# A two-block transformer kernel on one core: VectorE takes the conditioning tiles at every other step of a chunk

## The reference, cut to what matters

```
# block 1, feed-forward: D_FF = 5632
h = rmsnorm(x, pre_ffn_g)
u = causal_dwconv(h @ w_up, conv_w, conv_b)      # w_up: 2048 x 11264, 3 taps over tokens
gate, val = split(u)
x = x + rmsnorm((gelu(gate) * val) @ w_down, post_ffn_g)

# block 2, its six modulation vectors: w_ada is 2048 x 12288 (100 MB)
m = silu(cond) @ w_ada + b_ada                   # cond: one vector; shift, scale and gate, twice
h = rms_norm(x, norm_w) * (1 + scale) + shift
...
x = x + g_m * (relu(hm @ w_mlp_up) ** 2 @ w_mlp_down)
```

## Time and profile before

| | |
|---|---|
| median of three executions | 2182.85 us |
| the profiled execution | 2189.57 us |
| its span, first to last instruction | 2187.9 us |
| TensorE busy | 2153.1 us, 98% |
| VectorE busy | 1529.7 us, 70% |
| ScalarE busy | 1085.6 us, 50% |
| GpSimd busy | 133.3 us, 6% |
| read from HBM | 483.00 MB, 222 GB/s over the span |

### The profile page before, as it was taken

One profiled execution on the slowest core, in us unless ns is written; L12 is line 12 of the kernel. 1 busy time (PEld: TensorE's weight loads), 2 busy tenths in 40 slices (PEclk: granted clock), 3 DMA queues, 4 the chain that ended last, 5 costly groups with the idle time before them and its releaser, 6 DMA issues.

```text
span 2187.9 us, 32356 instructions
## 1 busy us (share of the span) xinstructions
PE 2153.1 (98%) x10220; PEld 1780.4 (81%) x10220; DVE 1529.7 (70%) x1906; ACT 1085.6 (50%) x1458; POOL 133.3 (6%) x233
## 2 busy tenths in 40 slices
PE   8999999999999999999999999999999999999998
PEld 7888888888778888788888878888888888888876
DVE  7997779787897887867877554566555655555656
ACT  6545654655334554345588465464434434444434
POOL 2110000100010000100000000000000000000000
PEclk9999899999999999999999999999999999999999
DMA  9887077788898888978666541558667766766653
GB/s 331 290 271 251 3 246 245 252 269 276 259 289 268 276 270 265 308 237 265 220 218 195 174 154 49 176 170 273 209 194 231 221 194 205 240 194 210 227 172 111
DMA packets 279982, 487.05 MB, mean 223 GB/s; under 512 B 26252, under 2 KB 118740, under 8 KB 278560
## 3 DMA queue, kind: packets, MB, share of 16 engines
q1 hardware_dynamic: 249472, 371.42, 51.9%
q0 software_dynamic: 30192, 113.72, 17.1%
q10 hardware_dynamic: 176, 0.08, 0.0%
HBM read 483.00 MB, written 2.11 MB: 222 GB/s over the span
## 4 chain that ended last, share of the span: by engine, by line
PE 95%; ACT 2%; DVE 1%; issue 1%; DMA 0%; POOL 0%; ACTq 0%; POOLq 0%
PE G L1883 28%; PE G L1885 28%; PE G L1884 28%; PE T L2151 1%; PE T L2303 1%; PE T L2072 1%; ACT w_hi L583 1%; PE G L2052 1%; PE T L1917 1%; PE G L2283 1%; PE T L2097 0%; PE T L1965 0%; PE T L2099 0%; PE T L2098 0%; PE G L1980 0%
## 5 line engine op out<-in xcount | busy, mean ns | idle before, releaser
L1096 DVE TENSOR_TENSOR w_lo<-raw,w_hi 128x1024 fp32r<-128x1024 f32 (+1 forms) x704 | 849.0, 1216 | 445.1 <-ACT w_hi L583 442.3
L583 ACT ACTIVATE w_hi<-raw 128x1024 fp32r<-128x1024 f32 (+1 forms) x704 | 740.2, 1055 | 818.4 <-PE G L1885 812.0
L1883 PE MATMUL G<-w_hi,h_hi 128*128 128x512 f32 (+1 forms) x1656 | 648.1, 391 | 3.2 <-DVE h_lo L1181 1.9
L1885 PE MATMUL G<-w_hi,h_lo 128*128 128x512 f32 (+1 forms) x1656 | 642.4, 388 | 0.6 <-issue 0.6
L1884 PE MATMUL G<-w_lo,h_hi 128*128 128x512 f32 (+1 forms) x1656 | 641.7, 387 | 0.0
L1883 PE MATMUL G<-w_hi,a_hi 128*128 128x512 f32 x1120 | 440.7, 394 | 10.4 <-issue 6.8
L1885 PE MATMUL G<-w_hi,a_lo 128*128 128x512 f32 x1120 | 436.9, 390 | 0.0
L1884 PE MATMUL G<-w_lo,a_hi 128*128 128x512 f32 x1120 | 436.6, 390 | 0.0
L1883 PEld LDWEIGHTS G<-w_hi,h_hi 128*128 128x128 f32 x1656 | 311.5, 188 | 67.7 <-issue 6.6
L1885 PEld LDWEIGHTS G<-w_hi,h_lo 128*128 128x128 f32 x1656 | 311.1, 188 | 64.3
L1884 PEld LDWEIGHTS G<-w_lo,h_hi 128*128 128x128 f32 x1656 | 311.4, 188 | 61.5
(11 more groups left out here) (280 smaller groups left out, 1245.6 us busy)
## 6 DMA issues: line engine op xcount, KB each, us to landing
ada_w<-in_w_ada POOLq DMA_DIRECT2D x192, 512.0 KB, 5.0
raw<-in_w_up SPq DMA_DIRECT2D x352, 256.0 KB, 4.4
raw<-in_w_mlp_up SPq DMA_DIRECT2D x256, 256.0 KB, 2.9
raw<-in_w_mlp_down SPq DMA_DIRECT2D x256, 256.0 KB, 3.4
raw<-in_w_in SPq DMA_DIRECT2D x224, 256.0 KB, 4.0
raw<-in_w_down SPq DMA_DIRECT2D x176, 256.0 KB, 4.7
raw<-in_w_out SPq DMA_DIRECT2D x128, 256.0 KB, 3.8
raw<-in_w_in SPq DMA_DIRECT2D x16, 136.0 KB, 3.5
```

What stands on the lines that cost most here:

```text
L583: act.activation(w_hi[:, s % 4, :, 0:width], raw[:, s % 8, :, 0:width], ACT.Copy).then_inc(hi_ready, 1)
L1096: dve.tensor_tensor(w_lo[:, s % 4, :, 0:width], raw[:, s % 8, :, 0:width], w_hi[:, s % 4, :, 0:width].bitcast(F32), ALU.subtract).then_inc ...
L1883: pe.matmul(out, ah, wh, start=f, stop=False)
L1885: mm = pe.matmul(out, al, wh, start=False, stop=l)
```

## The change

`body` no longer spreads the tiles evenly over the steps that it has left. A table gives, for each number of tiles in a chunk, the steps behind whose low part they stand; they no longer keep to k of 4 and above in a chunk with taps and product.

| tiles in the chunk | before | after |
|---|---|---|
| 4, with taps and product | 4, 5, 6, 7 | 1, 3, 5, 7 |
| 4, without | 0, 1, 2, 3 | 1, 3, 5, 7 |
| 3 (up1c) | 4, 5, 6 | 1, 4, 6 |
| 2 (second feed-forward part) | 4, 5, or 0, 1 in a group's first chunk | 1, 5 |
| 1 (first chunk of up1c) | 0 | 4 |
| 6 (first chunk of up1b) | 0 to 5 | 0, 1, 3, 4, 6, 7 |
| the chunks that start at k = 5 | 5, 5, 6, 7 and 5, 6 | the same |

The tiles keep their order, the folds their steps, and no other stream is touched.

```
+        TILE_AT = {1: (4,), 2: (1, 5), 3: (1, 4, 6), 4: (1, 3, 5, 7), 6: (0, 1, 3, 4, 6, 7)}
+
         def body(s, d=0, post=None, n=8, adas=(), k0=0, fold=()):
 
-            adas = list(adas)
+            at = {2: (5, 6), 4: (5, 5, 6, 7)}[len(adas)] if k0 else TILE_AT.get(len(adas), ())
             for k in range(k0, n):
                 lo(s + 3 + k, d)
                 for at_, v, half in fold:
                     if at_ == k:
                         ada_fold(v, half)
-                if post and k == 2:
-                    post[0]()
-                elif post and k == 3:
-                    post[1]()
-                elif not post or k >= 4:
-                    left = n - k if not post else n - max(k, 4)
-                    for _ in range(-(-len(adas) // left)):
-                        ada_op(*adas.pop(0))
+                if post and k in (2, 3):
+                    post[k - 2]()
+                for a, op in zip(at, adas):
+                    if a == k:
+                        ada_op(*op)
```

## The result

| | before | after |
|---|---|---|
| median | 2183.61 us (2181.55 to 2188.32, 6 runs) | 2170.52 us (2169.48 to 2173.88, 6 runs) |
| ratio | | 0.9938, 95% interval 0.9924 to 0.9952 |
| span of the profiled execution | 2187.9 us | 2167.7 us |

The kernel after is 0.6% faster, 13.1 us by the medians; 2172 were forecast. The spans of the two profiled executions differ by 20.2 us, and that number must not be read as the gain. Both kernels run the same instructions up to the first transposes of up1a, and there the one before had already lost 7.4 us: they start at 407.37 in it, and at 399.93 in the kernel after. The windows over the attention of the first block show why (the row's columns are those of the earlier trace rows, with the granted clock third from the end).

What follows compares the result with a forecast made beforehand. TensorE, busy 98% of the span, was taken as the bound, losing time to VectorE's order. Gaps of -13.5 us and a fold wait of +2.2 gave -11.3, taken as -10.8 from 2182.85: 2172 us, range 2168 to 2181.

Steps and rivals of the forecast that it cites:

- The bound, and the loads behind the gaps: Whole kernel: TensorE sets the end; VectorE's 78.8 us of waits for tile loads cause TensorE's gaps, 13.5 us at stake.
- the gap at 548: Up1a: a TensorE gap of 0.54 us before a matmul at 548.03, expected to go, worth 0.8 us.
- The yardstick: Step costs: TensorE 2.72 us a step; VectorE 1.14 for a low part, 2.39 for a two-instruction tile, 1.20 for one.
- the 5.6 us of allowed lateness: Feed-forward steps: VectorE may be 5.6 us late with its low parts before TensorE waits.
- Down1a, -8.4: Down1a, 16 two-instruction tiles: VectorE enters on time, no gap is left, about 8.4 us saved.
- The fold in up1b, +2.2: Up1b's first chunk: the fold before step 3 newly waits 2.3 us for late tiles, costing 2.0 to 2.6, taken as 2.2.
- the case that holds it: Rival at up1b's fold: wait of 2.9 us and half clock behind it, total -9.4 us, 2173.5 us; chance 0.12.
- Up1a, -0.8, and down1b, -4.5: Up1a loses its one gap, 0.8 us; down1b's gaps come of loads alone and go, 4.5 us.
- Up1c and the second feed-forward part, 0: Up1c and the second feed-forward part: no gaps in the rows, so nothing gained; 0, bounds -0.5 to +1 us.
- The sum: All stages: -13.5 + 2.2 = -11.3 us on the profiled execution; -10.8 taken for the runs' median.
- quick loads: Rival: unprofiled loads land in 3.7 us, VectorE hardly waits before the change; gain only 2 us, 2181 us; chance 0.15.
- The slower rival: Chunks with taps, 14: early tiles meet a late VectorE, 1.2 us lost in each, total 2202 us; chance 0.05.

Runs made afterwards that it cites:

- e5: Kernel before, with the 112 tiles from up1a to up1c taken but not loaded and no wait for loads; 0.9945 of before, down1a 117.97 us.
- e6: Kernel after, with the same 112 tiles from up1a to up1c taken but not loaded; 0.9930 of before, down1a 115.77 us.
- e3: Kernel before, with the new tile steps in the up chunks of all three groups and none in the down chunks; 0.9968 of before.
- e1: Kernel before, with the new tile steps in the four chunks of down1a alone; 0.9987 of before (interval takes in 1), down1a 123.25 us.
- e4: Kernel after, with the second part's fold in up1b's first chunk moved from steps 3 and 5 to 5 and 7; 0.9931 of before.
- e9: Kernel after, with the tiles of down1a's last chunk at k = 0, 2, 4, 6; 0.9948 of before, fold wait 0.65 us.
- e7: The kernel after again, unchanged: a slip left the intended new steps unused, so it serves as a repeat; 0.9941 of before, down1a 115.78 us.
- e8: The kernel after again, unchanged: a slip left the intended new steps unused, so it serves as a repeat; 0.9938 of before, down1a 117.43 us.
- e10: Kernel after, with the four tiles of a chunk that has taps at k = 0, 1, 2, 3; 0.9986 of before, 2177.4 us.
- e2: Kernel before, with the new tile steps in down1b alone; 0.9986 of before (interval takes in 1), down1b 116.53 us.

## Why the prediction was right

*The bound, and the loads behind the gaps.* Right. 3.57 us of idle time in down1b and the gap at 548 are gone, VectorE's waits fell from 78.8 to 2.9 us (under 15 forecast), and e5 and e6 show that it is the loads. In down1a they hold the larger part and the row of tiles the rest, as the working had it. The waits were counted from 407 us on, and so the forecast misses the one that loads cause ahead of the first transposes; the change leaves it as it was.

*The yardstick* held: 3.5 us for a tile of two and a low part is the distance of e3's gaps, and the 5.6 us of allowed lateness gave e3's 4.7 us and e1's 3.4 us ahead of time (4 to 5 and 3 expected).

*Down1a, -8.4.* Without the fold it has no gap left, as forecast. The length fell by 5.4 us, 122.75 to 117.39. With the fold out of the way (e4, 113.37) it is 9.4 us shorter, and 0.5 of these are the old fold's wait: 8.9 for the term of 8.4.

*The fold in up1b, +2.2.* The wait is 2.23 us in the profile after, where the working gave 2.3 without a late load; against 0.27 that is +2.0. The place, the tile at k = 7, is shown by e9. The part of it that e4 gives back is 2.4 us, against 0.5 before: +1.9. I left the half clock out of the forecast, with a chance of 0.12 for the case that holds it. Of six profiled executions with this wait of 2.2 us (after, e1, e6, e7, e8, e10) four have it and two don't: 117.4 against 115.8 us for down1a. That it should come only where two gaps stand close together was wrong.

*Up1a, -0.8, and down1b, -4.5.* Measured -0.99 and -4.91. That the loads alone cause the gaps of down1b is right (e5). Where they do it was half right: by e2 and e3, one profile each, a part of the lateness came with VectorE out of up1b, and not from the tiles inside the stage. In the whole change both go, so the sum didn't notice.

*Up1c and the second feed-forward part, 0.* Up1c went from 113.37 to 113.33 us; in the rest of the kernel, 1107.6 us before and 1106.2 after, no gap came or went that a tile ends.

*The sum.* The stages from up1a to up1c fell by 11.3 us in the profiled pair, the forecast's own sum. That they agree so closely is luck: the gaps were worth 14.8 us where 13.5 were put at stake, the fold took back 1.9 instead of 2.2, and the half clock, left out of the sum, took back 1.6. Without it the stages would have fallen by 12.9. (A slip in the working hardly matters: it counts restarts for 10 gaps, none of them the fold's, and then takes the fold's 0.24 out of their sum.) The medians say 13.1, with an interval of 10.5 to 16.6. The step to the median was argued wrongly: I put a part of the 6.7 us by which the profile of before lay above it down to slower loads. That profile had 7.4 us more behind it than the one after before the first changed instruction, by half clock in the attention stage. And over the 66 executions of the kernel before that ran beside the experiments the time goes with the mean granted clock: 2191.3 us in the mean of the four at 0.992, the clock of that profile, and 2182.4 us for the 15 at 0.996. That leaves little for "quick loads".

*The slower rival.* Its mechanism exists (a late load at k = 1 in e2, too little room ahead of the taps for two-instruction tiles in e10), but needs VectorE to be late when it comes to the early tile, which the new order itself prevents: no chunk with taps of the kernel after has a gap.

## What to carry to other kernels

When a side job shares an in-order engine with the feed of the bottleneck, its place is set by two clocks: its own loads (two buffers mean that a tile can be taken only as often as twice per load time) and the slack of the feed. Rows of side work break both, and a wait on a load at the end of one stage may be paid in the next; count the lateness on through the stages, against the number of steps that the buffers allow. Count the waits from ahead of the stage that you change: the load wait ahead of the first transposes, 1.6 us in the kernel after, was in no stage and stayed. And wherever a tile moves later, look at who waits for the last one: here 1.9 of 14.8 us went back to a fold whose step in the same table could have moved along.

## What the runs showed of the hardware that was not expected

The clock is granted at half speed for 3.4 us behind some waits of TensorE and not behind others of the same length in the same kernel: behind the fold's 2.2 us in four executions of six; behind a gap of 2.35 us at 578 us in e1, but behind none of the gaps in down1a of e2, the longest of which was 2.51 us, nor behind the one of 2.31 us at 581 us in e10. Of the 13 waits of TensorE above 2 us that stand between 395 and 1109 us in the 13 profiles, nine had it behind them and four had not. Each time it cost about 1.6 us. And the attention stage runs at half clock for a time that differs between executions of the same instructions (mean clock 0.88 and 0.95 over 100 us), which moves the span by some 7 us, as much as half of this change: of two kernels that close, stage lengths between two fixed instructions tell more than spans.
